# Down matrices in two passes over column halves, with 2x2 block products made of seven block products in two of every eight slots

## The reference

```python
# first block
h = rmsnorm(x, norm_mlp_pre[l])
f = jnp.square(jax.nn.relu(h @ w_ff1[l])) @ w_ff2[l]
x = x + rmsnorm(f, norm_mlp_post[l])
# second block
m = rmsnorm_2(h, norm_mlp[l]) @ w_up[l]
h = h + jnp.square(jax.nn.relu(m)) @ w_down[l]
...
return rmsnorm_2(h, final_norm)
```

## Time and profile before

| | |
|---|---|
| median of 3 runs | 2256.61 us (2256.32 to 2257.11) |
| the profiled execution | 2256.06 us, its span 2254.3 us |
| TensorE busy | 2231.1 us, 99% of the span |
| vector engine busy | 1331.8 us, 59% |
| scalar engine busy | 1040.1 us, 46% |
| first down matrix | products issued from 788.6 to 1136.6 us |
| second down matrix | products up to 2240.6 us |

### The profile page before, as it was taken

One profiled execution on the slowest core, in us unless ns is written; L12 is line 12 of the kernel. 1 busy time (PEld: TensorE's weight loads), 2 busy tenths in 40 slices (PEclk: granted clock), 3 DMA queues, 4 the chain that ended last, 5 costly groups with the idle time before them and its releaser, 6 DMA issues.

```text
span 2254.3 us, 32839 instructions
## 1 busy us (share of the span) xinstructions
PE 2231.1 (99%) x13276; PEld 1918.3 (85%) x13276; DVE 1331.8 (59%) x1548; ACT 1040.1 (46%) x1453; POOL 93.2 (4%) x66
## 2 busy tenths in 40 slices
PE   8999999999999999999999999999999999999998
PEld 7888988888888888888898988888888888888887
DVE  6878665764545555444486578847545455444445
ACT  6433564643434444444464476635434344434344
POOL 0552000000000000000000000000000000000000
PEclk9999999999999999999999999999999999999999
DMA  8464435566666555565554433365666665555553
GB/s 323 128 153 157 150 131 218 165 187 186 186 187 187 188 200 188 209 237 186 193 165 137 166 113 113 134 200 155 186 187 187 187 187 193 194 189 200 189 191 107
DMA packets 153513, 402.32 MB, mean 178 GB/s; under 512 B 15296, under 2 KB 30912, under 8 KB 133200
## 3 DMA queue, kind: packets, MB, share of 16 engines
q1 hardware_dynamic: 142112, 394.83, 53.3%
q10 hardware_dynamic: 11312, 6.22, 1.2%
HBM read 398.90 MB, written 2.13 MB: 178 GB/s over the span
## 4 chain that ended last, share of the span: by engine, by line
PE 95%; DVE 3%; ACT 1%; DMA 0%; issue 0%; SPq 0%; ACTq 0%; DVEq 0%
PE ps L757 21%; PE ps L760 11%; PE ps L797 10%; PE ps L798 10%; PE ps L799 10%; PE ps L620 5%; PE ps L628 3%; PE ps L629 3%; PE ps L630 3%; PE ps L999 2%; PE ps L1000 2%; PE ps L1001 2%; PE ps L642 2%; PE ps L644 2%; PE ps L643 2%; PE ps L1097 1%
## 5 line engine op out<-in xcount | busy, mean ns | idle before, releaser
L2299 DVE TENSOR_TENSOR w_low<-raw_weights,w_high 128x1024 fp32r<-128x1024 f32 x659 | 776.5, 1218 | 774.0 <-ACT w_high L1502 770.7
L1502 ACT ACTIVATE w_high<-raw_weights 128x1024 fp32r<-128x1024 f32 (+1 forms) x634 | 634.8, 1049 | 812.7 <-PE ps L799 398.5
L757 PE MATMUL ps<-x_split,w_high 128*128 128x512 f32 x2048 | 558.7, 394 | 1.7 <-DVE x_split L2287 1.7
L799 PE MATMUL ps<-w_high,x_split 128*128 128x512 f32 x1024 | 398.4, 389 | 0.0
L798 PE MATMUL ps<-w_low,x_split 128*128 128x512 f32 x1024 | 398.4, 389 | 0.0
L797 PE MATMUL ps<-w_high,x_split 128*128 128x512 f32 x1024 | 398.4, 389 | 0.0
L757 PEld LDWEIGHTS ps<-x_split,w_high 128*128 128x128 f32 x2048 | 350.0, 188 | 48.4 <-issue 3.0
L760 PEld LDWEIGHTS ps<-x_split,w_low 128*128 128x128 f32 x2048 | 313.7, 188 | 44.4
L760 PE MATMUL ps<-x_split,w_low 128*128 128x256 f32 x2048 | 325.8, 281 | 0.0
L799 PEld LDWEIGHTS ps<-w_high,x_split 128*128 128x128 f32 x1024 | 192.3, 188 | 40.0
L797 PEld LDWEIGHTS ps<-w_high,x_split 128*128 128x128 f32 x1024 | 192.3, 188 | 39.9
(11 more groups left out here) (298 smaller groups left out, 2316.7 us busy)
## 6 DMA issues: line engine op xcount, KB each, us to landing
raw_weights<-in_w_ff SPq DMA_DIRECT2D x128, 1024.0 KB, 5.6
raw_weights<-in_w_up SPq DMA_DIRECT2D x64, 1024.0 KB, 5.7
raw_weights<-in_w_down SPq DMA_DIRECT2D x64, 1024.0 KB, 4.8
raw_weights<-in_w_in SPq DMA_DIRECT2D x62, 1024.0 KB, 5.3
raw_weights<-in_w_out SPq DMA_DIRECT2D x32, 1024.0 KB, 4.8
raw_weights<-in_w_mem_kv SPq DMA_DIRECT2D x7, 1024.0 KB, 15.1
residual<-in_xT SPq DMA_DIRECT2D x2, 2048.0 KB, 13.9
region<-t_table ACTq DMA_DIRECT2D x1, 3072.0 KB, 16.8
```

The costliest lines, as they stand in the source:

```text
L757: nc.tensor.matmul(o, wh[:, q, w], xs[:, kt], start=(kt == 0), stop=False, skip_group_check=True)
L799: last = nc.tensor.matmul(o, l, wh[:, r], start=False, stop=True, skip_group_check=True)
L1502: nc.scalar.activation(split_slot(wh_t, k)[:, r], ring_slot(n)[:, r], ACT.Copy).then_inc(rounded, 1)
L2299: V.tensor_tensor(split_slot(wl_t, k)[:, r], ring_slot(n)[:, r], split_slot(wh_t, k)[:, r].bitcast(f32), ALU.subtract).then_inc(split_read ...
```

## The change

Each slot of a down matrix becomes 256 rows by 1024 columns, still 1 MB. The matrix is worked through twice: the first four passes of the loop take all rows of the left 1024 columns, the other four all rows of the right ones. The hidden activations are split anew in each half, two tiles (512 columns) per slot.

Within a body of eight slots, slots 0, 1, 3, 4, 6 and 7 are *plain*: 4 banks (2 token halves x 2 column blocks) x 2 row tiles x 3 matmuls = 24, into banks 4 to 7. Slots 2 and 5 are *summed*: the 2x2 blocks (token halves x row tiles, and row tiles x column blocks) are multiplied in Winograd's form, seven block products of 3 matmuls, of which one goes to bank 0 alone, and others to banks 1 to 3 and 4 to 7. The fifteen sums: four of 128-column activation blocks and four of 512-column weight blocks before each summed slot (`sums`, seven vector instructions, as one makes two of the weight sums), and seven block sums at the end of each half (`combine` and the additions with banks 4 to 7). Raw operands and sums are split into high and low as before; summed slots have buffers of their own (`raw_high`, `sums_w`, `sums_x`), laid over parts of `x_split`, `mixed`, `residual` and `rinv`, so the double buffer serves the plain slots alone.

On the vector engine the sums of slot 2 stand at the head of a body and those of slot 5 between slots 3 and 4. At the end of a half the scalar engine copies bank 0 to `home` (`first_product`) once slot 5 is used, the vector engine adds banks 2, 3 and 1 (`combine`), and then adds banks 4 to 7 (`keep`) behind the lows of the next half's slot 0. TensorE waits for each of these before it starts a bank again. At the end of `ff2_1` the left half is copied and squared ahead (`home_row`), and four banks are left (`whole`, `whole_square`); at the end of `ff2_2` the left half gets its residual ahead (`final_left`), the residual of the right one is added to `home` (`final_ahead`), and four banks are left. The load of the bias table moves behind the sixth pass.

```diff
@@ sync queue @@
-                        sp.dma_start(ring_slot(n0 + j), w[bass.ds(i * (BODY * P) + P * j, P), :]).then_inc(slot_loaded[(n0 + j) % RING], 16)
+                            src = w[bass.ds(i * (2 * BODY * P) + (2 * P * j - back), 2 * P), c0:c0 + 1024]
+                            sp.dma_start(ring_slot(n0 + j).rearrange("p (k c) -> p k c", k=2),
+                                         src.rearrange("(k p) c -> p k c", p=P)).then_inc(slot_loaded[(n0 + j) % RING], 16)
@@ TensorE @@
+                def summed(i, j, begins):
...
+                    def product(bank, x, wh, wl, r):
+                        x, r, o = slice(P * x, P * x + P), slice(512 * r, 512 * r + 512), ps[:, bank, :]
+                        begin = starts and bank < 4
+                        nc.tensor.matmul(o, sh[:, x], wh[:, r], start=begin, stop=False, skip_group_check=True)
+                        nc.tensor.matmul(o, sh[:, x], wl[:, r], start=False, stop=False, skip_group_check=True)
+                        return nc.tensor.matmul(o, sl[:, x], wh[:, r], start=False, stop=True, skip_group_check=True)
...
+                    pe.wait_ge(sums_ready, i * 8 + (4 * s + 1))
+                    pe.wait_ge(split_ready, i * (2 * BODY) + (2 * k + 1))
+                    product(7, 2, raw_high, raw_low, 2)
+                    product(0, 0, raw_high, raw_low, 0)
+                    pe.wait_ge(sums_ready, i * 8 + (4 * s + 3))
+                    product(6, 6, raw_high, raw_low, 1)
+                    product(1, 3, th, tl, 0)
+                    product(3, 5, th, tl, 1)
+                    pe.wait_ge(sums_ready, i * 8 + (4 * s + 4))
+                    product(2, 4, th, tl, 2)
+                    pe.wait_ge(split_ready, i * (2 * BODY) + (2 * k + 2))
+                    product(5, 1, th, tl, 3).then_inc(split_used, 1)
@@ scalar engine @@
+            def plain(name, i, j, later):
...
+                act.wait_ge(split_used, i * BODY + (SPLIT0[name] + PLAIN_BEFORE[j] + 1))
+                act.wait_ge(gains_loaded, 16)
+                nc.scalar.activation(pair_x[c % 2][0], pair_of(i, j, later), ACT.Copy).then_inc(chunk_rounded, 1)
+                act.wait_ge(slot_loaded[n % RING], i * (16 * BODY // RING) + 16 * (n // RING + 1))
+                for h in range(2):
+                    r = slice(SLOT // 2 * h, SLOT // 2 * (h + 1))
+                    nc.scalar.activation(split_slot(wh_t, k)[:, r], ring_slot(n)[:, r], ACT.Copy).then_inc(rounded, 1)
+            def summed(name, i, j, later):
...
+                nc.scalar.activation(sums_x[0][:, 0:384], pair_of(i, j, later, P, 384), ACT.Copy).then_inc(sums_rounded, 1)
+                act.wait_ge(slot_loaded[n % RING], i * (16 * BODY // RING) + 16 * (n // RING + 1))
+                nc.scalar.activation(raw_high, w[:, 512:2048], ACT.Copy).then_inc(rounded, 1)
+                act.wait_ge(sums_made, i * 14 + (7 * s + 2))
+                nc.scalar.activation(th[:, 0:1024], scr[:, 0:1024], ACT.Copy).then_inc(sums_rounded, 1)
+                act.wait_ge(sums_made, i * 14 + (7 * s + 5))
+                nc.scalar.activation(th[:, 1024:1536], scr[:, 1024:1536], ACT.Copy).then_inc(sums_rounded, 1)
+                act.wait_ge(sums_made, i * 14 + (7 * s + 6))
+                nc.scalar.activation(sums_x[0][:, 384:896], scr[:, 1536:2048], ACT.Copy).then_inc(sums_rounded, 1)
+                act.wait_ge(sums_made, i * 14 + (7 * s + 7))
+                nc.scalar.activation(th[:, 1536:2048], w[:, 0:512], ACT.Copy).then_inc(rounded, 1)
@@ vector engine @@
+                def sums(i, j, later=False):
...
+                    V.tensor_tensor(s1, x[0], x[2], ALU.add).then_inc(sums_made, 1)
+                    dve.wait_ge(slot_loaded[n % RING], i * (16 * BODY // RING) + 16 * (n // RING + 1))
+                    V.tensor_tensor(t13, w[:, 0:3:2], w[:, 1::-1], ALU.subtract).then_inc(sums_made, 1)
+                    V.tensor_tensor(s3, x[1], x[0], ALU.subtract).then_inc(sums_made, 1)
+                    dve.wait_ge(sums_made, i * 14 + (7 * s + 1))
+                    V.tensor_tensor(s2, s1, x[1], ALU.subtract).then_inc(sums_made, 1)
+                    dve.wait_ge(sums_made, i * 14 + (7 * s + 2))
+                    V.tensor_tensor(t2, w[:, 2], t1, ALU.subtract).then_inc(sums_made, 1)
+                    dve.wait_ge(sums_made, i * 14 + (7 * s + 4))
+                    V.tensor_tensor(s4, x[3], s2, ALU.subtract).then_inc(sums_made, 1)
+                    dve.wait_ge(sums_made, i * 14 + (7 * s + 5))
+                    V.tensor_tensor(w[:, 0], w[:, 3], t2, ALU.subtract).then_inc(sums_made, 1)
...
+                def body(i, later=False):
+                    sums(i, 2, later)
+                    plain(i, 0, later)
+                    plain(i, 1, later)
+                    rest(i, later)        # summed 2, plain 3, sums 5, plain 4, summed 5, plain 6, plain 7
...
+                with dve.Fori(1, HALF_ITERS) as i:
+                    body(i)
+                combine(name, HALF_ITERS)
+                sums(HALF_ITERS, 2, True)
+                plain(HALF_ITERS, 0, True)
+                for b in range(4):
+                    keep(name, b)
+                plain(HALF_ITERS, 1, True)
+                rest(HALF_ITERS, True)
+                with dve.Fori(HALF_ITERS + 1, FF2_ITERS) as i:
+                    body(i, True)
```

More of the change, by code:

```diff
@@ L2382, in down @@
                 last_summed()
[L2383 removed]
+                plain(0, 1)
                 last_squared()
[L2385 to L2392 removed]
+                rest(0)
+                with dve.Fori(1, HALF_ITERS) as i:
+                    body(i)
```

357 lines of the change are left out of this document (247 added, 110 removed).

## The result

The changed kernel takes 2240.97 us (median of 4 runs, 2240.66 to 2241.43), the kernel before 2256.47 in the same series: ratio 0.9932, 95% interval 0.992 to 0.9943. In the profiled executions the span falls from 2254.3 to 2239.4 us, by 14.9 us, where the sum of the steps gave 19.9. Sign and mechanism are as forecast; 5 us of the gain are missing, and the experiments ask where they went.

A forecast was written before the change was run, and what follows sets the result against it. TensorE's number of matmuls was taken as the bound. Terms -21.8 + 0.2 + 0.2 + 0.4 + 1.1 = -19.9 us took 2256.06 to 2236.2, given as 2237 for the runs' median; range 2233 to 2249.

The forecast's parts named there:

- What goes: Summed slots of both down matrices: 3 matmuls fewer in each of 32, 96 x 0.2267 = 21.8 us saved.
- matmuls spaced wider: Profile sign that the forecast is wrong: matmuls further apart than the 0.227 us spacing expected; no chance given.
- rival 1: Loop of the down matrices stalls in part, 0.5 to 0.6 us per pass; about 2246 (2241 to 2252), chance 0.17.
- What comes beside TensorE: Vector and scalar work per loop pass, 34.9 and 23.2 us of 42.17: both still fit, 0 lost in the loop.
- u: Extra cost of each short or waiting instruction in the loop's chain of 37.3 + 30u us; taken 0.03, at most 0.18.
- The cover: Loop: slack of the 37.3 + 30u us chain against the 42.17 us pass, about 4 us; nothing lost while it lasts.
- Starts and passes: Start of each down matrix and change between column halves: 0.1 us lost each, ranges 0 to 0.5 and 0 to 0.7.
- End of the first matrix: Behind the first down matrix: two squares in a row on the scalar engine, +0.4 us (-0.3 to +1).
- End of the kernel: Behind the second matrix: first turning product at +1.95 after the end, second group 1.2 later; +1.1 us (0 to +2.5).
- Rival 2: In-order vector queue in the loop becomes the bound, kernel slower; 2279 us at u = 0.25, chance 0.08.

## Why the prediction was nearly right

- *What goes.* Right in number (2976 matmuls instead of 3072), wrong in price. The step "186 x 0.2267 = 42.17 us, a summed slot 4.76" took the spacing of the earlier trace rows over to matmuls whose stationary operands lie elsewhere. They measured 232 ns; the term was -21.8 and came to -17.5. That is nearly the whole miss (4.25 of 5), and no bound or rival held it: the step had a price without a range, and "matmuls spaced wider" stood only among the signs of being wrong. That the measured 2240.97 still lies within the range, at the border between the forecast (2233 to 2241) and rival 1 (2241 to 2252), is in part luck: the range reached so high for stalls of the loop, and there were none. When the errors were moved, the very 337.2 us and 4.760 us of the forecast came out, with the same products.
- *What comes beside TensorE.* 34.3 us of vector and 23.8 of scalar work in a pass, against 34.9 and 23.2. The instructions of the sums came cheaper than taken: in the loop the next instruction starts 0.60 us behind one of 512 columns (I had 0.64) and 0.20 behind one of 128 (0.24; the rows at 930.97 above), so u was about 0. By the rule that the Trainium skill gives on the page "VectorE: DVE Perf Modes", section "The DRAIN you can't avoid", u would have been 0.11; the trace does not agree, since instructions recorded as 0.68 us start 0.60 us apart. The section makes an exception that the prediction passed over, that a next operation which is not held starts earlier, and the trace agrees with that. The cover "about 4 us" held in the loop at +3.6 and was gone at +7.3, where the pass was 45.2 us for a computed 44.6. A load of 4 KB rows took 5.7 us (5.5 taken).
- *Starts and passes.* 0.17 us a matrix (0.1 each and 0.1 between the passes taken; between them nothing was lost). Right.
- *End of the first matrix.* +0.44 for a forecast +0.4. The diagonals were done 0.90 and 3.43 us behind the products, for +0.75 and +3.45, and the turning starts at 0.96 and 3.49. Right; a mere reordering takes most of it back.
- *End of the kernel.* +1.5 for +1.1, within 0 to 2.5. The first turning was at +2.50 (1.95 forecast), the second group 1.6 later than before (1.2 forecast). The mechanism, four squares ahead of the first block's copy, was in the text, and the run that changes it takes the whole excess away.
- *Rivals.* None of the stalls came. Rival 2 names the right bound: with the vector work raised by 7.3 us a pass the kernel is slower than before (2294.6), through the in-order vector queue behind the wait for a load.

What stays open: why a summed slot with this operand at the high end is slow even on a multiple of 64 bytes. The gain of the seven products themselves isn't in doubt: with all slots plain it is gone.

## What to carry to other kernels

When TensorE is the bound and work is cut from it, the new matmuls' price is read from matmuls with operands in the same places, or given a bound of its own: 5 to 6 ns in 227 took a fifth of the 21.8 us here. Put stationary operands where this kernel's fast ones lay, on a multiple of 128 bytes near the ones in use, and give the odd corners to scratch that no matmul reads. Before two runs are compared at 1 us, look at the granted clock: one fall of 3.4 us to the 1.2 GHz level cost 1.2 us between the matrices. A cover counted in a steady loop says nothing of its first pass and of the kernel's end; there, look which short copy stands in a queue behind work that nobody waits for.

## What the runs showed of the hardware

- The spacing of 512-column matmuls with 128x128 stationary operands depends on where one stationary operand in three is read from: 226.7 ns near the others on a multiple of 128 bytes; 233 there at an odd multiple of 32 bytes (4.890 us for 21); 231 at the high end on a multiple of 128 (4.854); 232 there at an odd multiple of 32 (4.872). Neither the order of the PSUM banks nor counted waits that are already met between the products changed it by 1 ns (4.872 us in all three kernels).
- The slowness lags: it reaches up to eight matmuls past the last such operand, also across a change of slot (4.833 us and seven uneven spacings behind it with the places exchanged).
- A fall of the granted clock to the 1.2 GHz level for 3.4 us (18 matmuls of 256 columns in place of 29) came in 5 of 14 profiled kernels at the same place between the matrices and cost 1.2 us. In the 13 us ahead TensorE was busy 12.0 both in the kernel with the banks in order, where it fell, and in the changed kernel, where it did not.
- Vector instructions recorded as 0.68 us follow one another at 0.60 us, those recorded as 0.28 us at 0.20, also when each waits for a count that has been reached.
